# The router of a mixer and experts layer: squares summed in the mixer's tail, logits in column strips, four position products, picks and gates made pair by pair inside the experts

## What is computed

```python
xf = rmsnorm(h, norm2_w) * (1 + sc2) + sh2          # 512 x 1024
def expert_choice_ffn(xn, router_w, w_gate, w_up, w_down):
    cap = CAPACITY_FACTOR * n // N_EXPERTS            # 64 slots an expert, 16 experts
    logits = jnp.einsum('bnd,de->ben', xn, router_w).astype(jnp.float32)
    aff = jax.nn.softmax(logits, axis=1)              # over the experts
    gate, idx = lax.top_k(aff, cap)                   # each expert picks its 64 tokens
    xg = jax.vmap(lambda xs, ix: xs[ix])(xn, idx)
    hid = jax.nn.silu(einsum(xg, w_gate)) * einsum(xg, w_up)
    y = einsum(hid, w_down) * gate[..., None]
    # y is added back at the picked tokens
h = h + g2 * expert_choice_ffn(xf, ...)
```

## Time and profile before

| | |
|---|---|
| time, median of 3 runs | 3527.58 us (3526.75 to 3527.63) |
| time of the profiled execution | 3521.8 us |
| its span | 3520.0 us |
| TensorE busy | 3229.8 us, 92% of the span |
| VectorE, ScalarE, GpSimd busy | 1330.5, 1067.6, 289.1 us |
| mean granted TensorE clock | 0.961 of 2.4 GHz |

### The profile page before, as it was taken

One profiled execution on the slowest core, in us unless ns is written; L12 is line 12 of the kernel. 1 busy time (PEld: TensorE's weight loads), 2 busy tenths in 40 slices (PEclk: granted clock), 3 DMA queues, 4 the chain that ended last, 5 costly groups with the idle time before them and its releaser, 6 DMA issues.

```text
span 3520.0 us, 37656 instructions
## 1 busy us (share of the span) xinstructions
PE 3229.8 (92%) x14986; PEld 2263.9 (64%) x14986; DVE 1330.5 (38%) x1829; ACT 1067.6 (30%) x1777; POOL 289.1 (8%) x241
## 2 busy tenths in 40 slices
PE   6878899986999997999999999998999999989996
PEld 3546677864444434775677768876766677768874
DVE  3246444332001014554434443334464433443334
ACT  2127233221000003444533232212444533232212
POOL 0018120001000001110110000000111110000000
PEclk9997999997999998999999999999999999999998
DMA  6010343333999993111122222233211112212231
GB/s 235 0 48 1 132 156 131 115 141 156 409 409 409 409 402 96 61 52 46 43 66 88 80 72 96 88 90 77 83 49 50 36 61 84 96 63 93 92 91 57
DMA packets 266253, 436.72 MB, mean 124 GB/s; under 512 B 9696, under 2 KB 180192, under 8 KB 265312
## 3 DMA queue, kind: packets, MB, share of 16 engines
q1 hardware_dynamic: 265936, 432.41, 34.9%
q0 software_dynamic: 144, 1.90, 0.1%
HBM read 432.19 MB, written 2.10 MB: 123 GB/s over the span
## 4 chain that ended last, share of the span: by engine, by line
PE 53%; DVE 4%; ACT 2%; DVEq 1%; issue 1%; ACTq 0%; DMA 0%; POOLq 0%; SPq 0%; POOL 0%
PE bank L2126 44%; PE bank L2187 2%; PE bank L2204 1%; PE bank L2223 1%; PE bank L2163 1%; PE bank L1776 1%; DVE ring_r L2458 1%; PE bank L2218 1%; ACT ring_r L2327 1%; PE bank L2193 1%; DVE x L1807 0%; DVE layers_norm_rstd L1804 0%; DVE layers_work L2577 0%; DMA ring<-in_w_in 0%; DVE x_r L1818 0%
## 5 line engine op out<-in xcount | busy, mean ns | idle before, releaser
L2126 PE MATMUL bank<-experts_x_hi_r,ring_r 128*128 128x512 f32 x1720 | 574.6, 399 | 7.0 <-DVE ring_r L2458 7.0
L2126 PE MATMUL bank<-x_r,ring_r 128*128 128x512 f32 x1376 | 545.4, 396 | 0.0
L2458 DVE TENSOR_TENSOR ring_r<-ring,ring_r 128x2048 fp32r<-128x2048 f32 (+2 forms) x162 | 324.3, 2002 | 429.5 <-ACT ring_r L2327 428.5
L2327 ACT ACTIVATE ring_r<-ring 128x2048 fp32r<-128x2048 f32 (+2 forms) x162 | 272.6, 1683 | 497.0 <-PE bank L2126 476.4
L2126 PE MATMUL bank<-layers_work_r,ring_r 128*128 128x512 f32 x1312 | 392.5, 401 | 9.2 <-DVE layers_work_r L2601 9.2
L2126 PEld LDWEIGHTS bank<-experts_x_hi_r,ring_r 128*128 128x128 f32 x1720 | 323.0, 188 | 108.6 <-issue 25.2
L2126 PE MATMUL bank<-ring_r 128*128 128x512 f32 (+1 forms) x1224 | 387.2, 377 | 0.0
L2126 PEld LDWEIGHTS bank<-layers_work_r,ring_r 128*128 128x128 f32 x1312 | 249.9, 191 | 78.4 <-DVE layers_work_r L2601 10.0
L2126 PEld LDWEIGHTS bank<-x_r,ring_r 128*128 128x128 f32 x1376 | 258.6, 188 | 62.4 <-issue 1.0
L2650 POOL TENSOR_TENSOR layers_p<-layers_p,layers_recip 128x512 f32<-128x512 f32 (+2 forms) x160 | 145.1, 923 | 1449.2 <-DVEq L2504 1449.2
L2126 PEld LDWEIGHTS bank<-ring_r 128*128 128x128 f32 x1224 | 223.8, 188 | 46.5
(11 more groups left out here) (371 smaller groups left out, 4644.4 us busy)
## 6 DMA issues: line engine op xcount, KB each, us to landing
ring<-in_w_in SPq DMA_DIRECT2D x74, 1024.0 KB, 5.3
ring<-in_w_ffn_in SPq DMA_DIRECT2D x44, 1024.0 KB, 5.1
ring<-in_w_gate SPq DMA_DIRECT2D x30, 1024.0 KB, 18.4
ring<-in_w_down SPq DMA_DIRECT2D x28, 1024.0 KB, 18.5
ring<-in_w_up SPq DMA_DIRECT2D x26, 1024.0 KB, 17.9
mixer_kept<-in_w_down SPq DMA_DIRECT2D x24, 1024.0 KB, 18.5
mixer_kept<-in_w_up SPq DMA_DIRECT2D x23, 1024.0 KB, 18.0
mixer_kept<-in_w_gate SPq DMA_DIRECT2D x22, 1024.0 KB, 18.5
```

What stands on the lines that cost most here:

```text
L2126: last = pe.matmul(out, lhs, rhs, start=start and k == 0, stop=stop and k == len(pairs) - 1)
L2327: act.activation(r32(whole(key, hi_at(i, key))), whole(key, raw_at(i, key)), ACT.Identity).then_inc(slab_round, 1)
L2458: dve.tensor_tensor(r32(tile), tile, r32(hi), ALU.subtract).then_inc(done, 1)
```

## The change

The squares are made in the mixer: as soon as tile m of `core.x` is written, ScalarE squares it into the free `gate` tiles and VectorE adds it to a running sum in an unused part of the weight ring (`square_sum`). The router then needs one product for the mean. A one-column square root ahead of the real one makes ScalarE load its table early. The logits are made the other way round: `router_w`, padded to 32 columns with zeros by GpSimd, is stationary, and `xf` tile k streams by it as it comes, into column strip k mod 4 of the array; four transposes and one reduction add the four strips up. The transposes of the softmax now stand ahead of those of `xf`. The positions take four products in place of ten. In the router only the picks of pair 0 are made. Those of pairs 1 to 7, all gates, their transposes and copies are made inside `experts`, the transposes between the gather and the turn of each pair.

```diff
+def square_sum(core):
+    return core.ring[:, :, :].rearrange("p a b -> p (a b)")[:, IN_RING * EXPERT_PIECE:IN_RING * EXPERT_PIECE + T]
...
 (mixer, scalar)
+                        elif n == "wo":
+                            m = 4 * s + j
+                            act.wait_ge(x_new, m + 1)
+                            act.activation(gate[:, m % 4, :], core.x[:, m, :], ACT.Square).then_inc(squared, 1)
 (mixer, vector)
+            def add_square(m):
+                dve.wait_ge(squared, m + 1)
+                if m:
+                    dve.tensor_tensor(square_sum(core), square_sum(core), gate[:, m % 4, :], ALU.add)
+                else:
+                    dve.tensor_copy(square_sum(core), gate[:, 0, :])
+                dve.drain()
...
+                        dve.drain().then_inc(x_new, 1)
+                        if j:
+                            add_square(m - 1)
+                if n == "wo":
+                    add_square(4 * s + 3)
...
+def pick_pair(dve, core, b, p):
+    pair = [P, TT, 2, CAP]
+    return dve.tensor_tensor(b.pick[:, :, p * P:(p + 1) * P].rearrange("p t (e s) -> p t e s", s=CAP),
+                             core.c("slot").unsqueeze(1).unsqueeze(1).broadcast_to(pair),
+                             b.pos[:, :, 2 * p:2 * p + 2].unsqueeze(3).broadcast_to(pair), ALU.is_equal)
...
 (router, sync)
-            sp.dma_start(rw[:, :, :], w_tiles(I["router_w"], 0, D, 0, EXPERTS)).then_inc(rw_in, 16)
+            sp.wait_ge(rw_zero, 1)
+            sp.dma_start(rw[:, :, 0:EXPERTS], w_tiles(I["router_w"], 0, D, 0, EXPERTS)).then_inc(rw_in, 16)
 (router, tensor)
             core.banks.vacant(pe, "rms")
-            for k in range(KD):
-                pe.wait_ge(sq_done, k + 1)
-                last = pe.matmul(core.ps("rms")[:, :], core.c("mean_d"), sq[:, k % 2, :], start=k == 0, stop=k == KD - 1)
+            pe.matmul(core.ps("rms")[:, :], core.c("mean_d"), square_sum(core), start=True, stop=True)\
+                .then_inc(core.banks.put("rms"), 1)
+            pe.wait_ge(rw_in, 16)
+            core.banks.vacant(pe, "strips")
             for k in range(KD):
+                pe.wait_ge(xf_done, k + 1)
+                rows = slice(CPAD * (k % 4), CPAD * (k % 4) + CPAD)
+                last = pe.matmul(core.ps("strips")[rows, :], rw[:, k, :], xf[:, k, :], start=k < 4, stop=k >= 4)
+            last.then_inc(core.banks.put("strips"), 1)
+            pe.wait_ge(strips_kept, 1)
             core.banks.vacant(pe, "logits")
             for t in range(TT):
-                last = product(pe, core.ps("logits")[:, t * EXPERTS:(t + 1) * EXPERTS],
-                               [xf[:, k, t * P:(t + 1) * P] for k in range(KD)], [rw[:, k, :] for k in range(KD)])
+                last = pe.transpose(core.ps("logits")[:, t * P:(t + 1) * P], strips[:, t * P:(t + 1) * P], core.c("ident"))
...
-            for t in range(TT):
-                last = product(pe, core.ps("pos")[:, t * EXPERTS:(t + 1) * EXPERTS],
-                               [core.c("ones")] * t + [core.c("tri_f")], [mask[:, j, :] for j in range(t + 1)])
+            pe.matmul(core.ps("pos")[:, 0:TT * EXPERTS], core.c("tri_f"), mask[:, :, :], start=True, stop=False)
+            for t in range(1, TT):
+                last = pe.matmul(core.ps("pos")[:, t * EXPERTS:TT * EXPERTS], core.c("ones"), mask[:, 0:TT - t, :],
+                                 start=False, stop=t == TT - 1)
...
 (router, scalar)
-                act.activation(sq[:, k % 2, :], core.x[:, k, :], ACT.Square).then_inc(sq_done, 1)
+            act.activation(warm[:, :], core.c("eps6"), ACT.Sqrt)
...
+            core.banks.filled(act, "strips")
+            act.activation(strips[:, :], core.ps("strips")[:, :], ACT.Identity).then_inc(core.banks.done("strips"), 1)
 (router, vector)
-            dve.tensor_copy(aff[:, :, :], core.ps("logits")[:, 0:TT * EXPERTS].rearrange("p (t e) -> p t e", e=EXPERTS))\
+            four = core.ps("logits")[:, :].rearrange("p (t j e) -> p t e j", t=TT, j=4)[:, :, 0:EXPERTS, :]
+            dve.tensor_reduce(aff[:, :, :], four, AX.X, ALU.add).then_inc(core.banks.done("logits"), 1)
...
-            for t in range(TT):
-                dve.tensor_tensor(b.pick[:, t, :].rearrange("p (e s) -> p e s", s=CAP),
-                                  core.c("slot").unsqueeze(1).broadcast_to([P, EXPERTS, CAP]), over(pos[:, t, :]),
-                                  ALU.is_equal).then_inc(pick_done, 1)
+            pick_pair(dve, core, b, 0)
...
 (router, gpsimd)
+            pool.memset(rw[:, :, :], 0.0).then_inc(rw_zero, 1)
...
 (experts, banks 6 and 7)
-        mixed += [("xg", i + 1, hh) for hh in (0, 1)] * (i + 1 < PAIRS) + [("ht", i, hh) for hh in (0, 1)]
+        mixed += [("xg", i + 1, hh) for hh in (0, 1)] * (i + 1 < PAIRS) + [("put", i)] + [("ht", i, hh) for hh in (0, 1)]
 (experts, tensor)
+            def placed(i):
+                pe.wait_ge(gates_done, i + 1)
+                mix_banks.vacant(pe, ("put", i))
+                for t in range(TT):
+                    last = pe.transpose(mix_ps(("put", i))[:, t * P:(t + 1) * P], gates[:, i % 2, t, :], core.c("ident"))
+                last.then_inc(mix_banks.put(("put", i)), 1)
...
                 if i + 1 < PAIRS:
+                    pe.wait_ge(pick_done, i + 1)
                     gather(i + 1)
+                placed(i)
                 turn(i)
 (experts, scalar)
+                mix_banks.filled(act, ("put", i))
+                act.activation(b.put[:, i, :], mix_ps(("put", i))[:, :], ACT.Identity).then_inc(mix_banks.done(("put", i)), 1)
+                act.drain().then_inc(put_done, 1)
 (experts, vector)
+            for i in range(1, PAIRS):
+                pick_pair(dve, core, b, i).then_inc(pick_done, 1)
 (experts, gpsimd)
+            for i in range(PAIRS):
+                if i:
+                    pool.wait_ge(pick_done, i)
+                if i >= 2:
+                    mix_banks.filled(pool, ("put", i - 2))
+                pool.tensor_tensor(gates[:, i % 2, :, :].rearrange("p t (e s) -> p t e s", s=CAP),
+                                   b.pick[:, :, i * P:(i + 1) * P].rearrange("p t (e s) -> p t e s", s=CAP),
+                                   b.aff[:, :, 2 * i:2 * i + 2].unsqueeze(3).broadcast_to([P, TT, 2, CAP]), ALU.mult)\
+                    .then_inc(gates_done, 1)
```

83 lines of the change are left out of this document (30 added, 53 removed).

## The result

The changed kernel takes 3479.55 us (median of four, 3477.88 to 3482.5), the one before 3527.52 in the same comparison: 48.0 us less, a ratio of 0.9865 with a 95% interval of 0.9848 to 0.9882. Its profiled execution took 3482.5, with a span of 3480.7.

The account below looks back on a forecast made before the run. The router was taken as a chain of latencies and the experts as bound by DMA from about the third pair. The router's -38.75 us and the gather's +2.2 gave -36.5, so 3527.58 became 3491.1, range 3485 to 3500.

Parts of the forecast that it names:

- mixer's tail: Behind the mixer's last write of `x`, a square, the last addition and handovers were to add 1.5 us.
- norm to reciprocal: From router start to reciprocal, only one product and the root were to be left: 2.9 us for 10.75, saving 7.8.
- logits: In the router, strips beside the scaling were to leave 3.8 us behind the last shift, saving 9.9 of 13.88.
- picks, gates, transposes, copies: At the router's end, one pick of 1.0 us and handovers, 1.6 in all, were to replace 18.93, saving 17.3.
- gather to first expert product: The first gather was to start at TensorE's lower clock and cost 2.2 us more, with bounds of 0 and 7.4.
- Inside the experts, 0: Picks and transposes moved into the experts were to cost nothing, covered by TensorE's waits for weights; without cover +5.3 us.
- Rival 1: TensorE bounds the experts after all, so 0.66 us of each pair is paid, 5.3 in all: 3496 us; chance 0.13.
- rival 2: TensorE's clock stays low through the first gather, 5.2 us more: 3496 us; chance 0.06.
- rival 3: The strips' products in the router don't run beside each other, 7 us more: 3498 us; chance 0.06.
- Rival 5: Slower than before: the clock falls ahead of the gather and stays at 1.2 GHz into the experts' matrices; chance 0.02.
- Rival 4: More is saved, 39 to 41 us, by no clock cost and a faster norm and strips: 3487 to 3489; chance 0.09.
- the saving is taken from it unchanged: Last step: the sum of -36.5 us was taken from the whole kernel's median of 3527.58, giving 3491.1.

Follow-up runs that it names:

- squares_back: The changed kernel with the squares, their eight products and the table load back in the router; 3494.49 us, chain 55.6 us.
- strips_back: The changed kernel with the logits made as before, `xf` stationary and a copy in place of the reduction; 3497.46 us, chain 61.2 us.
- picks_back: The changed kernel with all picks, gates, transposes and copies back in the router; 3504.21 us, chain 65.8 us.
- placed4: The changed kernel with each pair's four gate transposes issued four times over, 12 more a pair; its experts took 485.9 us.
- end17: The changed kernel with an idle 1.7 us reciprocal of 256 columns behind the last write of the experts' block; 3485.47 us, ratio 0.9894 to the kernel before.
- before_later17: The kernel before with an idle reciprocal of 256 columns, about 1.7 us, ahead of the router's picks; 3517.94 us, ratio 0.9977.
- before_later34: The kernel before with an idle reciprocal of 512 columns, 3.35 us, ahead of the router's picks; 3520.94 us, ratio 0.9988.
- before_end34: The kernel before with an idle reciprocal of 512 columns, 3.35 us, behind the last write of the experts' block; 3523.47 us, ratio 1.0006.

## Why the prediction was wrong

**What held.** The steps of the chain, each as an interval in the trace before and after:

| step | forecast | measured | how |
|---|---|---|---|
| mixer's tail | +1.5 | +1.7 | 1.94 from last write to router, 0.27 before |
| norm to reciprocal | -7.8 | -7.9 | 2.88 in place of 10.75 |
| logits | -9.9 | -10.9 | 2.83 from last shift to reduction in place of 13.93, +0.2 for the reduction's 0.42 in place of a copy of 0.22 |
| softmax's transposes | -2.65 | -2.4 | 4.00 - 0.2 in place of 6.21 |
| positions | -2.6 | -2.6 | 1.92 in place of 4.48 |
| picks, gates, transposes, copies | -17.3 | -17.65 | 1.32 in place of 18.97 |
| gather to first expert product | +2.2 | +1.5 | 9.61 in place of 8.11 |
| sum | -36.5 | -38.2 | 87.11 to 48.88 |

Three terms were mis-sized. The logits gave 1.0 more: I had taken the last product and the four transposes at the lower clock throughout, and in this stretch the clock was partly up, 0.50 from 784 to 788, 0.83 to 790 and 1.00 to 791 (the transposes took 0.66 in place of 0.84, the last record ended 1.42 behind the last shift in place of 1.9). The gather paid 1.5 and not 2.2. And a pick of 512 columns costs 0.69, not 1.0: of the four picks of 1024 columns in the earlier trace rows the first two take 1.22 each, and the last two, which start while GpSimd is at the gates, 2.92, so that an eighth of the row was no price for a pick without GpSimd at work. squares_back, strips_back and picks_back show the three big terms one by one: 6.6, then 10.9 and 1.3 in the gather, then 16.8.

**Inside the experts, 0** came out as 0.3 to 1.6 (483.4 and 484.5 against 482.9 and 483.1). The cover that I named is real: placed4 hid about 8 of 10.5 us behind the weights. Rival 1, 5.3 us, is out. So is rival 2, since the clock rose in the gather of the changed kernel, and rival 3, since the strips ended 1.42 behind the last shift. Rival 5 did not occur. Rival 4, with more saved in norm and strips, was the right direction for the chain: 38.2 against its 39 to 41. No rival had a time below 3487, so none of them has what happened.

**The step that failed** is the last one: "the saving is taken from it unchanged". It takes for granted that all outside the chain costs the same in both kernels, and that the three executions of before stand for its usual time. That the rest costs the same is what failed: the time fell by 48.0 and the chain by 38.2, and the experts did not shrink. The baseline may have failed as well. In the one other comparison that has both kernels they lie 47.7 apart (3525.91 and 3478.17), so the difference is no accident of the first. But the kernel before ran 77 times over all comparisons, with a median of 3524.5 and executions from 3517.4 to 3529.3; the 3527.52 of the comparison in the result lie 3.0 above. Each of the later comparisons ran on a chip of its own, and those in which it stood at 3524.4 and 3523.0 did not have the changed kernel, so whether the 3.0 are chance or the chip is open. The changed kernel ran eight times, median 3478.8 (3476.9 to 3487.0). Between the pooled medians are 45.7 us. The part that the chain doesn't hold is therefore 7.5 by the pooled medians and 9.5 by the second comparison.

It goes with the clock. The mean granted clock is 0.960 before and 0.966 changed, which is 282 and 237 us at 1.2 GHz, 45 less (a unit in the last digit is 7 us). In the traces the chain accounts for some 24 of them: its clock is 0.67 over 87.1 us and 0.65 over 48.9. The other 21 lie in code that did not change; as an estimate, a busy TensorE gains some 10 us by them, and 7.5 to 9.5 were to be explained.

The delays say whether that is a matter of the removed work or of where a kernel happens to stand. Take each delay's median, subtract its kernel in the same comparison (for end17 the 3478.8 of two others; the kernel before stood 1.5 below its pooled median beside end17, so the +6.7 is rather too small) and its own length (1.7, 3.3 or 5.1):

| delay | kernel before | changed kernel |
|---|---|---|
| 1.7 in the router | -8.0 - 1.7 = -9.7 | +6.6 - 1.7 = +4.9 |
| 1.7 behind the experts | -2.6 - 1.7 = -4.3 | +6.7 - 1.7 = +5.0 |
| 3.3 in the router | -2.0 - 3.3 = -5.3 | |
| 3.3 behind the experts | +0.5 - 3.3 = -2.8 | |
| 5.1 in the router | +1.6 - 5.1 = -3.5 | +12.0 - 5.1 = +6.9 |
| mean | -5.1 | +5.6 |

By the medians every delay of the kernel before cost less than it is long, and every delay of the changed kernel more. The first stands in a bad place, in which TensorE spends more time at the lower clock than after a small shift, the second in a good one. With both moved off their places the difference is 45.7 - 5.1 - 5.6 = 35.0, or 37.0 from the 47.7 of the same comparison, against 38.2 less the 1 of the experts. This is an estimate from small numbers. The three of the changed kernel rest on four executions each, which spread over 7 to 8 us and overlap with those of the changed kernel, and 0.9 of each of its two delays in the router are the slower gather. For the kernel before, the intervals of before_later17 and before_later34 lie below 1 by themselves, and all but that of before_end34 end below the delay's own length.

**Shown:** added idle time makes the kernel before faster by up to 8 us, and the time of its executions goes with their granted clock; in the one trace of that delay the layers are shorter, with the same records of TensorE busy for 6.4 us less (2032.6 against 2039.0) and a higher clock in the stretches shown. The layers of the changed kernel lie on that side as well: 2173.7 to 2176.6 in eight traces of it and its variants of the same router, against 2173.9 to 2181.6 in seven of before and its delays; the two ranges overlap. **Open:** what ties the places to the start, and whether the router's own length has a part in it: picks_back, with the long end of the router back, has layers of 2177.4 in its one trace, between the two kernels. A delay acts from the router and from behind the experts, but not equally, single executions of the kernel before differ by up to 12 us, and in the traces an early last write of `x` (766.4 to 769.4) goes with long layers (2177.9 to 2181.6) in the kernel before, but not in the changed one (2173.7 to 2176.6 with 768 to 774). Of the executions of a comparison only one has a trace.

## What to carry to other kernels

A stretch where one engine works at a time can be costed row by row from the trace: seven terms between 1 and 17 us came out within 1 us each. What can't be had from a trace is where the rest of the program will stand afterwards: with many short stalls of TensorE, unchanged stages move by some 5 us with any shift, in either direction, once by nearly 10, so such a forecast needs that much added on both sides of its range, and a baseline of more than three executions. Which way this program would move I could not have said beforehand. Before crediting a change with a few tenths of a per cent outside the lines it touches, run both kernels with a few microseconds of idle time put in.
